# A third of the expert weight loads issued from ScalarE's queue in a one-core hybrid decoder step

## The reference

```python
logits = (t @ w_router + b_router).astype(jnp.float32)
top_v, top_e = lax.top_k(logits, TOP_K)          # 4 of 32
gates = jax.nn.softmax(top_v, axis=-1)
...
def expert_block(args):
    xb, e = args
    hh = xb @ w1[e] + b1[e]                      # 1024 -> 2048
    glu, lin = jnp.split(hh, 2, axis=-1)
    glu = jnp.minimum(glu, SWIGLU_LIMIT)
    lin = jnp.clip(lin, -SWIGLU_LIMIT, SWIGLU_LIMIT)
    act = glu * jax.nn.sigmoid(SWIGLU_ALPHA * glu) * (lin + 1.0)
    return act @ w2[e] + b2[e]                   # 1024 -> 1024
```

## Time and profile before

| | |
|---|---|
| median of 3 runs | 1239.72 us (1238.82 to 1240.23) |
| profiled execution | 1238.85 us, its span 1237.0 us |
| PE busy | 1150.5 us (93%) |
| DVE, ACT busy | 418.7 us (34%), 251.2 us (20%) |
| SP's queue (q1) | 455.36 MB, 89.9% of 16 engines' span |
| ScalarE's queue (q10) | 4.54 MB, 1.2% |
| expert loads | 192 of 2048 KB, all from SP's queue |

### The profile page before, as it was taken

How to read it: one execution, slowest core, us unless ns; L and a number is a source line. 1 busy time by engine, 2 the same in 40 slices (tenths; PEclk the granted TensorE clock), 3 DMA queues, 4 the chain that set the end, 5 groups by cost and what they waited for, 6 DMA issues and landing times.

```text
span 1237.0 us, 16619 instructions
## 1 busy us (share of the span) xinstructions
PE 1150.5 (93%) x6725; PEld 585.7 (47%) x6725; DVE 418.7 (34%) x745; ACT 251.2 (20%) x415; POOL 65.3 (5%) x99
## 2 busy tenths in 40 slices
PE   7998999997999999999998989898989898989996
PEld 6997899796434334343333333332323232323332
DVE  6769867477121222212121213122121212121214
ACT  4663244234101111110111011110101110111012
POOL 5302001132000000000000000000000000000000
PEclk9999999997999999999999999999999999999999
DMA  9464499996999999999999999999999999999994
GB/s 311 153 205 147 133 338 347 353 351 227 361 428 428 428 429 429 428 429 429 429 429 429 428 429 429 428 429 427 430 427 430 428 430 427 429 429 427 430 427 165
DMA packets 79749, 466.54 MB, mean 377 GB/s; under 512 B 4384, under 2 KB 51008, under 8 KB 54912
## 3 DMA queue, kind: packets, MB, share of 16 engines
q1 hardware_dynamic: 72816, 455.36, 89.9%
q0 software_dynamic: 1504, 6.13, 1.6%
q10 hardware_dynamic: 5392, 4.54, 1.2%
HBM read 460.32 MB, written 5.70 MB: 377 GB/s over the span
## 4 chain that ended last, share of the span: by engine, by line
PE 60%; DMA 31%; DVE 5%; ACT 2%; issue 1%; SPq 0%; ACTq 0%; DVEq 0%
DMA ring<-w 30%; PE bank L1802 21%; PE bank L1837 12%; PE bank L1454 8%; PE bank L1777 5%; PE bank L1757 4%; PE bank L1414 2%; PE bank L1589 2%; DMA ring<-w_in 1%; DVE split L909 1%; PE bank L1821 1%; ACT rest L830 1%; ACT split L593 1%; PE bank L1758 1%; PE bank L1649 1%
## 5 line engine op out<-in xcount | busy, mean ns | idle before, releaser
L1802 PE MATMUL bank<-ring,rest 128*64 128x512 f32 x2048 | 458.0, 595 | 38.2 <-DMA ring<-w 24.0
L1802 PEld LDWEIGHTS bank<-ring,rest 128*64 128x64 f32 x2048 | 143.6, 136 | 332.4 <-issue 267.4
L1837 PE MATMUL bank<-ring,rest 128*64 128x512 f32 x1024 | 226.8, 595 | 17.0 <-ACT rest L830 17.0
L1339 DVE TENSOR_SCALAR rest<-bank 128x512 f32<-128x512 f32 x32 | 22.1, 692 | 487.3 <-PE bank L1802 487.3
L1454 PE MATMUL bank<-split 128*128 128x288 f32 x928 | 151.5, 297 | 0.2 <-DVE split L1121 0.2
L1318 DVE TENSOR_TENSOR rest<-rest,bank 128x512 f32<-128x512 f32 (+1 forms) x102 | 66.9, 680 | 227.9 <-PE bank L1777 227.8
L1837 PEld LDWEIGHTS bank<-ring,rest 128*64 128x64 f32 x1024 | 71.2, 137 | 151.3 <-issue 134.9
L1454 PEld LDWEIGHTS bank<-split 128*128 128x128 f32 x928 | 134.0, 189 | 1.5 <-DVE split L1121 0.5
L826 ACT ACTIVATE rest<-rest 128x512 f32<-128x512 f32 x32 | 20.2, 631 | 523.7 <-DVE rest L1339 523.7
L1777 PE MATMUL bank<-rest 128*128 128x512 f32 (+1 forms) x204 | 98.4, 611 | 1.3 <-ACT rest L838 1.3
L838 ACT COPY rest<-bank 64x512 f32<-64x512 f32 x64 | 37.1, 580 | 225.3 <-PE bank L1837 224.5
(11 more groups left out here) (295 smaller groups left out, 753.1 us busy)
## 6 DMA issues: line engine op xcount, KB each, us to landing
ring<-w SPq DMA_DIRECT2D x192, 2048.0 KB, 33.5
ring<-w_in SPq DMA_DIRECT2D x12, 1024.0 KB, 7.3
ring<-k_t SPq DMA_DIRECT2D x8, 1024.0 KB, 12.6
ring<-v_c SPq DMA_DIRECT2D x8, 1024.0 KB, 7.7
ring<-w_xk SPq DMA_DIRECT2D x4, 1024.0 KB, 5.3
ring<-w_xv SPq DMA_DIRECT2D x4, 1024.0 KB, 6.6
ring<-w_out SPq DMA_DIRECT2D x4, 1024.0 KB, 7.2
ring<-w_xq SPq DMA_DIRECT2D x4, 1024.0 KB, 12.4
```

What stands on the lines that cost most here:

```text
L1802: last = t.matmul(out, slots[:, k, :], w[:, col], start=False, stop=(k == KT - 1))
L1837: last = t.matmul(ps[2][CAP * ds:CAP * ds + CAP, :], actT[:, at:at + CAP], w[:, b, 512 * ds:512 * ds + 512], start=(a == 0 and b == 0), st ...
```

## The change

Loads 2 and 10 of each expert leave SP's loop and are issued by ScalarE. ScalarE issues load 10 of the next expert between its wait for glu and the sigmoid, and load 2 of the expert after the next behind its two copies of the output; before each stands a wait for `units_used` with the same count as SP's. The prologue's eight loads stay with SP as they were, so of the other 184 loads 61 move. ScalarE's loop runs seven turns, and the last turn is written out behind it, without the loads of experts that do not exist. `one_round` is changed to match.

```diff
+ACT_LOADS = [2, 10]
...
             def turn(i, g, first=0):
                 for j in range(first, BODY * EXP_UNITS, 2):
+                    if j % EXP_UNITS in ACT_LOADS:
+                        continue
                     sp.wait_ge(units_used, g * (BODY * EXP_UNITS) + j + 1 - SLOTS + 1)
                     load_expert_units(sp, i * BODY, j)
...
-            def turn(g):
+            def load_behind(i, g, j, ahead):
+
+                load = EXP_UNITS * (j + ahead) + ACT_LOADS[2 - ahead]
+                act_e.wait_ge(units_used, g * (BODY * EXP_UNITS) + load + 1 - SLOTS + 1)
+                load_expert_units(a, i * BODY, load)
+
+            def turn(i, g, experts_left=2 * BODY):
                 for j in range(BODY):
                     n = g * BODY + j
                     act_e.wait_ge(glu_done, n + 1)
+                    if j + 1 < experts_left:
+                        load_behind(i, g, j, 1)
                     a.activation(sig, glu, ACT.Sigmoid, scale=ALPHA).then_inc(sig_done, 1)
...
                         a.copy(outp[j // 2][rows_e, half * 512:(half + 1) * 512],
                                ps[2][CAP * half:CAP * half + CAP, :]).then_inc(outp_done, 1)
-
-            with act_e.Fori(0, TURNS) as i:
-                turn(i)
+                    if j + 2 < experts_left:
+                        load_behind(i, g, j, 2)
+
+            def turns(g):
+
+                with act_e.Fori(0, TURNS - 1) as i:
+                    turn(i, g + i)
+                turn(TURNS - 1, g + TURNS - 1, BODY)
+            turns(0)
```

More of the change, by code:

```diff
@@ L847, in one_round @@
             def one_round(r):
-                with act_e.Fori(0, TURNS) as i:
-                    turn(r * TURNS + i)
+                for load in [n for n in range(SLOTS) if n % EXP_UNITS in ACT_LOADS]:
+                    act_e.wait_ge(units_used, r * (NE * EXP_UNITS) + load + 1 - SLOTS + 1)
+                    load_expert_units(a, 0, load)
+                turns(r * TURNS)
             def root_of_rows(tt):
```

## The result

The changed kernel takes 1245.54 us (median of 5 runs, 1245.34 to 1247.43); the kernel before took 1239.39 beside it (5 runs, 1237.72 to 1240.23). The ratio is 1.0055, 95% interval 1.0044 to 1.0066: 6.15 us slower by the medians, where +6.3 and 1246.0 were forecast; the ratio is formed from all the runs and stands for 6.8 us, its interval for 5.5 to 8.2. The profiled execution took 1246.94 us, its span is 1245.2 us.

A forecast was written before the change was run, and what follows sets the result against it. The DMA stream at 428 GB/s was taken to bound the kernel; issue costs and rate change counted 0, and landing order added 6.3 us to the 1237.0 span, giving 1243.3 and a median of 1246.0, range 1236 to 1252.

The forecast's parts named there:

- What bounds the kernel: Through the experts, the DMA stream at 427 to 430 GB/s sets the pace; TensorE waits for landings from 606.81 us.
- The order of landing: At the stream's end, ScalarE's loads overtake SP's, so expert 31's first matmul ends at 1217.73 instead of 1211.45: +6.3 us.
- The signs of being wrong: ScalarE loads landing in 30 us or more, middle rate outside 426 to 431, last landing over 2 us off 1217.5.
- ScalarE's loads in 9.8 us: On ScalarE's queue, each load gets about half the engines and lands some 9.8 us after its issue.
- ScalarE's issue in the sigmoid's cover: Between the glu wait and the sigmoid, load 10's issue takes 0.5 us, covered by 0.77 us before VectorE needs the result.
- the same 4.5 us: TensorE's waiting per two experts, 58.75 us of loads against 54.25 of work; claimed to hide 1.0 us from the table load.
- Rival 1: Engines serve ScalarE's packets behind SP's seven loads, so each load lands as before: 1239.7 us; chance 0.18.
- Rivals 2 and 3: Rate of two queues: more, 1232.3 us at 2.3%, chance 0.14; or 1 to 2% less, 1252 to 1258, chance 0.10.
- Rival 4: TensorE's clock drops after gathered waits, adding 1 to 2 us in the last two experts: 1247 to 1248; within the 0.58 case.

The follow-up runs named there:

- load 2 alone: Against the kernel before, ScalarE issues only load 2 of each expert and load 10 stays with SP: 1239.10 against 1238.64 us, ratio 1.0007.
- load 10 alone: Against the kernel before, ScalarE issues only load 10 of each expert and load 2 stays with SP: 1244.15 against 1238.64 us, ratio 1.0045.
- the last turn back: The changed kernel with all loads of the last four experts, 28 to 31, issued by SP again: 1239.64 us against 1238.64 for the kernel before, ratio 1.0008.
- only the last turn by ScalarE: The kernel before with only loads 2 and 10 of experts 28 to 31 issued by ScalarE: 1246.26 against 1238.64 us, ratio 1.0058.
- the issue behind the sigmoid: The changed kernel with load 10 issued after the sigmoid instead of ahead of it: 1246.38 us against 1239.58 for the kernel before, ratio 1.0055.
- the kernel with one split load: The kernel before with load 6 of expert 31 alone issued as two 1 MB transfers: 1237.44 against 1238.17 us, ratio 0.9991.

## Why the prediction was right, point by point

- **What bounds the kernel.** Right. From the twelfth slice to the last but one the stream moves 423 to 431 GB/s in every kernel of this study, with one queue or with two. Two readings were loose: the eleventh slice itself, with which the prediction begins, shows 361, and the stretch from 1217 to 1218 shows 0 GB/s, so the data had stopped before the 1217.54 that the sum gives; the last landing, 1182.26 + 35.3, bears the sum out.
- **The order of landing.** Right in mechanism and size. Counted from the traces: expert 31's first matmul ends 6.1 us ahead of the end of the stream before the change, 0.1 us behind it after. The same count, made ahead for the variants, came out within 0.1 us in the traces where a landing in the chain lets it be checked (load 2 alone, 4.8 us ahead of the stream's end for 4.7; load 10 alone, 1.2 for 1.2; the last turn back, 6.1 for 6.1). These ends are themselves counted from that landing, so the agreement shows which landing holds TensorE up and how many loads follow it. In the medians three variants came within 1 us: +0.5 for +1.4, +5.5 for +4.9 to 6.0, +1.0 for +1.1. Two came out higher: only the last turn by ScalarE +7.6 for +5 to 6.3, the issue behind the sigmoid +6.8 for +5.1 to 5.5; their intervals (5.6 to 8.8, 5.3 to 8.3) still reach into the forecasts.
- **The 8.2 us between the two profiled spans** are three things: 0.9 us lie ahead of the experts (the first gather matmul of expert 0's turn stands at 324.42 against 323.53, of no part of the change), 1.1 us are a later end of the stream (1219.58 - 0.9 against 1217.54), 6.2 us are the order. The prediction held the stream's end fixed, so that its 6.3 stands beside the 6.2 alone. That the medians differ by 6.15 and not by 7.3 is within their interval, 5.5 to 8.2 us, and that they agree with the forecast to 0.2 us is in part luck.
- **The signs of being wrong.** One of the three stands at its limit of 2 us: the last landing is 2.0 us off the 1217.5 that was named by its own landing time (1219.5), 2.1 by the count (1219.58). The later start and the later end of the stream just told make this up, not the order. ScalarE's loads stayed under 30 us and the rate between 426 and 431.
- **ScalarE's loads in 9.8 us.** Too small: 13.9, the one term that was clearly mis-sized. The share was right, but a load does not begin to move when it is issued. The queues of the changed kernel in a window right behind an issue at 1165.30 (1165.3 to 1168.3), and in one where both have work (1169 to 1177):

```profile
q1 hardware_dynamic: 84, 1.26, 98.8%
```

```profile
q10 hardware_dynamic: 111, 1.82, 53.3%
q1 hardware_dynamic: 105, 1.62, 47.6%
```

  In the first 3.0 us no packet of q10 appears; later the two share about evenly. The rows that the prediction read held such a delay already: by estimate half of 424 GB/s moves a store of 512 KB in 2.5 us, and the first landed after 6.0. The Trainium skill (DMA: Bandwidth & Descriptors, section Queues, rings and completion order) has each DMA engine go round between the queues that have work; the 53.3% and 47.6% agree. The count asked that load 2 of expert 31 be through when load 6 of expert 30 lands (1190.21). Its issue, another row of the timeline, came 14.2 us ahead of that and not 12.3, since it did not wait for the copies to end; 13.9 of landing leave 0.3. It also stood behind another load of its own queue, load 10 of expert 30, which landed at 1165.30 + 13.9 = 1179.2. The sum held by those 0.3 us, and by luck: two errors, 4.1 us in the landing and 1.9 us in the issue, met inside a slack of 2.5 us.

```profile
1176.02 0.33 ACTq L335 DMA_DIRECT2D ring<-w  x1
```

- **ScalarE's issue in the sigmoid's cover.** The issue took 0.33 to 0.37 us, not 0.5, and the cover held. The step that failed, in the first expert, is the one on the table load: "the same 4.5 us hide it" is true where TensorE waits for landings, not in expert 0, where the stream waits for TensorE to free slots. There the second matmul came 1.4 us later, and the DMA engines ran dry behind it (82 GB/s). The stream ends 1.1 us later, but that one made the other is not shown: the experiment behind the sigmoid did not show it, and the kernel with one split load has as late an end without it. The prediction had looked at that very spot for load 2 and not for the table load.
- **Rival 1, no change of order.** Out: 13.9 us to landing on ScalarE's queue against 29.7 on SP's.
- **Rivals 2 and 3, another rate.** Out: 427 to 430 GB/s in the slices. The rule of the Trainium skill (DMA: Bandwidth & Descriptors, section Rules for kernel authors) that spreading DMAs over issuing engines brings no bandwidth is borne out. What the prediction made of it taken alone, no change in the time, is not: 6.15 us.
- **Rival 4, the clock.** Real, and without weight in the end of the profiled execution. TensorE's waits for loads (total us, times, longest), first of the kernel before, then of the changed kernel:

```profile
PE bank L1802 <- DMA ring<-w: 24.0, 31, 1.2
```

```profile
PE bank L1821 <- DMA ring<-w: 30.7, 17, 3.3
```

In the changed kernel, the matmuls of a load behind two such waits, and the stretch in which the first of them ran:

```profile
632.12 5.35 PE L1821 MATMUL bank<-ring,rest 128*64 128x512 f32 x16 [3.17 <-DMA ring<-w]
...
1160.88 3.65 PE L1821 MATMUL bank<-ring,rest 128*64 128x512 f32 x16 [3.30 <-DMA ring<-w]
```

```profile
633.30:636.70 3.40, 3.40 (x10) 0.98 (x8) 0.00 (x0) 0.00 (x0) 0.00 (x0) 0.51 0.99 419
```

The waits have gathered, 17 of them and up to 3.3 us, for 31 of at most 1.2. Behind some of these the granted clock is 0.51 (1.2 GHz) and a load's matmuls take 5.35 us, 1.7 more than 3.65, as the prediction had it; behind others, as at 1160.88, it stays at 1.00 and they take 3.65. By the count above such a loss is made good from the 4.5 us a pair, unless it falls into the last experts, as in the run with the last turn alone. What it is worth in the medians was not tried.

## What to carry to other kernels

In this kernel, whose one stream of loads is bound by bandwidth, a second queue moved nothing faster but changed who was served next, and no order tried beat the order of use: each load that overtakes delays one that is waited for. The loss showed only at the end of the stream, so count it backwards, from the last landing through what the consumer still has to do; moving loads off the queue cost at most 2 us as long as the last four experts kept their order. A delay that waiting covers in the steady part should be looked at again where the stream itself runs dry, at its start: there the second matmul did come 1.4 us later, though what that cost in the end stays open.

## What the runs showed of the hardware that was not expected

- A load issued on ScalarE's queue at 1165.30, while SP's queue kept the engines busy (98.8%), had no packet in the first 3.0 us.
- A DMA issue put between a wait and the activation behind it moved the activation's table load behind that wait: 1.28 us went from a stretch of waiting into the path, once a turn, by an issue that itself takes 0.37 us.
- Waits of 3.17 and 3.33 us for a landing, in an engine otherwise busy, were followed by a granted clock of 0.51 (1.2 GHz): 5.35 and 6.40 us for matmuls that take 3.65. A wait of 3.30 us was followed by the full clock.
